# Norms between the matrix stages of a two-block transformer kernel, run in two token halves

## The reference, cut to what matters

```python
def rms_norm(x, g):
    return x * lax.rsqrt(jnp.mean(x * x, axis=-1, keepdims=True) + 1e-6) * g

def first_block(x, ...):
    x = x + 0.5 * g1 * swiglu(modulate(rms_norm(x, ffn1_norm), sh1, sc1), ...)      # FFN1
    h = modulate(rms_norm(x, mix_norm), sh2, sc2)                                   # norm 1
    x = x + g2 * (gated sum of a Fourier mix and a latent attention of h) @ w_out
    h = modulate(rms_norm(x, ffn2_norm), sh3, sc3)                                  # norm 2
    x = x + 0.5 * g3 * swiglu(h, ...)                                               # FFN2
    return rms_norm(x, final_norm)                                                  # norm 3

def second_block(x, ...):
    h = rms_norm(x, g_pre_mix) * (1 + sc1) + sh1                                    # norm 4
    o = concat(nsa_attention(h @ w_in ...), dsa_attention(...)) @ w_out
    x = x + gt1 * rms_norm(o, g_post_mix)                                           # norm 5
    h = rms_norm(x, g_pre_ffn) * (1 + sc2) + sh2                                    # norm 6
    y = square(relu(h @ w_up)) @ w_down                                             # FFN3
    return x + gt2 * rms_norm(y, g_post_ffn)                                        # norm 7
```

## Time and profile before

| | us |
|---|---|
| median of 3 runs | 2074.18 (2074.07 to 2074.76) |
| the profiled execution | 2074.3 |
| its span, first to last instruction | 2072.5 |
| TensorE (PE) busy | 1936.2 (93%) |
| DVE busy | 1212.3 (58%) |
| POOL busy | 1150.9 (56%) |
| ACT busy | 363.2 (18%) |
| chain that ended last: share of PE, DVE | 86%, 10% |

### The profile page before, as it was taken

One profiled execution on the slowest core, in us unless ns is written; L12 is line 12 of the kernel. 1 busy time (PEld: TensorE's weight loads), 2 busy tenths in 40 slices (PEclk: granted clock), 3 DMA queues, 4 the chain that ended last, 5 costly groups with the idle time before them and its releaser, 6 DMA issues.

```text
span 2072.5 us, 25215 instructions
## 1 busy us (share of the span) xinstructions
PE 1936.2 (93%) x8980; PEld 1526.7 (74%) x8980; DVE 1212.3 (58%) x1822; ACT 363.2 (18%) x749; POOL 1150.9 (56%) x1075
## 2 busy tenths in 40 slices
PE   6999999989899999899999978985999979999997
PEld 3788888868657888788888847664666748788785
DVE  7888478746644124887078355675774367405713
ACT  2100000022145111200000031112555230000001
POOL 3577777756440667576777643575000338767861
PEclk8999999999999999999999989896999989999998
DMA  8654555422220234454355221233000112233231
GB/s 277 203 175 158 189 167 183 151 85 89 64 62 1 62 102 140 129 189 132 118 191 172 89 68 41 81 72 93 1 1 1 41 41 87 95 101 94 89 101 40
DMA packets 231130, 216.51 MB, mean 104 GB/s; under 512 B 20305, under 2 KB 227342, under 8 KB 231054
## 3 DMA queue, kind: packets, MB, share of 16 engines
q1 hardware_dynamic: 230000, 214.84, 32.7%
q10 hardware_dynamic: 1054, 0.66, 0.1%
HBM read 213.39 MB, written 2.10 MB: 104 GB/s over the span
## 4 chain that ended last, share of the span: by engine, by line
PE 86%; DVE 10%; ACT 1%; issue 1%; POOL 1%; DMA 0%; ACTq 0%; DVEq 0%; POOLq 0%; SPq 0%
PE ps L614 24%; PE ps L616 24%; PE ps L615 23%; PE ps L891 5%; PE ps L914 4%; PE ps L900 3%; DVE rb L1437 1%; PE ps L660 1%; DVE tt L1931 1%; DVE tt L1654 1%; DVE xT L1932 1%; DVE ada_sum L1466 1%; DVE score L1815 1%; PE ps L645 1%; PE ps L851 0%
## 5 line engine op out<-in xcount | busy, mean ns | idle before, releaser
L525 POOL TENSOR_TENSOR w_lo<-raw,w_hi 128x512 fp32r<-128x512 f32 (+2 forms) x612 | 798.7, 1335 | 12.8
L614 PE MATMUL ps<-h_hi,w_hi 128*128 128x512 f32 x1424 | 565.6, 397 | 28.1 <-DVE h_lo L1459 26.7
L615 PE MATMUL ps<-h_lo,w_hi 128*128 128x512 f32 x1424 | 557.7, 392 | 0.0
L616 PE MATMUL ps<-h_hi,w_lo 128*128 128x512 f32 x1424 | 557.6, 392 | 0.0
L518 POOL TENSOR_TENSOR w_hi<-raw,ones 128x8 fp32r<-128x8 f32 x153 | 34.6, 226 | 870.1 <-PE ps L616 820.5
L614 PEld LDWEIGHTS ps<-h_hi,w_hi 128*128 128x128 f32 x1424 | 269.5, 189 | 92.0 <-issue 35.1
L1466 DVE SCALAR_TENSOR_TENSOR ada_sum<-ada,cT,ada_sum 128x256 f32<-128x256 f32 x378 | 325.1, 860 | 13.4
L615 PEld LDWEIGHTS ps<-h_lo,w_hi 128*128 128x128 f32 x1424 | 269.5, 189 | 58.0 <-issue 2.4
L616 PEld LDWEIGHTS ps<-h_hi,w_lo 128*128 128x128 f32 x1424 | 269.1, 189 | 57.8
L614 PE MATMUL ps<-g_hi,w_hi 128*128 128x512 f32 x608 | 237.4, 390 | 3.1 <-ACT sg L1396 3.1
L616 PE MATMUL ps<-g_hi,w_lo 128*128 128x512 f32 x608 | 236.7, 389 | 0.0
(11 more groups left out here) (274 smaller groups left out, 2239.3 us busy)
## 6 DMA issues: line engine op xcount, KB each, us to landing
ada<-in_ada_w SPq DMA_DIRECT2D x31, 1024.0 KB, 5.3
ada<-in_w_ada SPq DMA_DIRECT2D x24, 1024.0 KB, 6.6
raw<-in_ffn_w_gate SPq DMA_DIRECT2D x22, 1024.0 KB, 6.8
raw<-in_ffn_w_up SPq DMA_DIRECT2D x22, 1024.0 KB, 5.1
raw<-in_w_in SPq DMA_DIRECT2D x16, 1024.0 KB, 5.1
raw<-in_w_up SPq DMA_DIRECT2D x16, 1024.0 KB, 5.2
raw<-in_w_down SPq DMA_DIRECT2D x16, 1024.0 KB, 5.0
raw<-in_ffn_w_down SPq DMA_DIRECT2D x16, 768.0 KB, 4.3
```

The source lines that it names most:

```text
L525: last = pool.tensor_tensor(lo[:, c], src[:, c], hi[:, c].bitcast(F32), ALU.subtract)
L614: pe.matmul(o, wh, xh, start=start, stop=False)
L615: pe.matmul(o, wh, xl, start=False, stop=False)
L616: return pe.matmul(o, wl, xh, start=False, stop=stop)
```

## The change

Tokens 0 to 255 are half 0, tokens 256 to 511 half 1 (`HALF`). Two new functions on TensorE, with their counterparts on ACT (`boundary_high`) and DVE (`boundary`), replace the end of a stage and the start of the next:

- `last_pair`: output chunks 6 and 7 are computed for half 0 first, from the stage's last tile or last two tiles, then for half 1; the norm's sum of half 0 (`half_sum`) stands between the products of half 1.
- `first_tiles`: the first two tiles of the next stage are applied to half 0, then to half 1; the sum of half 1 stands after the fourth row chunk of the first of these tiles.
- DVE and ACT do the norm's root, reciprocal, scaling and split with 256 columns at a time; the reciprocal of half 1 stands in DVE's queue between the chunks of half 0.

This is done at norms 1, 2 and 4, and at norms 5 and 6 (there norm 6's sum over half 1, `mid_sum(1)`, stands behind half 0 of both first tiles); at norm 7 only the end of the stage is in halves, and the result is stored in halves, two chunks to a DMA.

Norms 3 and 4 are one: the root of mean(x²·g²) + 1e-6·(mean(x²) + 1e-6) is written as a sum of squares weighted by `gain2` = g² + 1e-6, and only one reciprocal goes into the scaling. The output of norm 3 itself, which the residual of block 2 needs, is computed later (`block1_root`, `block1_out`), between DVE's rotations and selections. For that TensorE does the plain sum of squares once more behind `first_tiles` of this norm (`y_sum`).

The first tile of each of the four stages behind such a norm (`EXTRA`: W_MIX, W_FFN2, W_IN2, W_FFN3) has a slot of its own (`we_hi`, `we_lo`); the other tiles alternate between the two old slots. The second tile of the stage goes into the slot of the tile two before it, as before, and the third tile into the slot of the last tile of the stage that ends. The rotations of `qi`, `kd` and `ki` move between the four token chunks of `nat`.

```diff
+EXTRA = (W_MIX, W_FFN2, W_IN2, W_FFN3)
...
+    we_hi = place("we_hi", [P, SLOT], F32R, at=at(20))
+    we_lo = place("we_lo", [P, SLOT], F32R, at=at(52))
...
+    def place_of(n):
+        return (n - sum(e < n for e in EXTRA)) % 2
...
+    def last_user(n):
+        return max(k for k in range(n) if k not in EXTRA and place_of(k) == place_of(n))
...
-            if not first:
+            if per:
                 pool.wait_ge(tile_used, i * per + (n - 1))
+            elif n in EXTRA:
+                pool.wait_ge(tile_used, n - 3)
+            elif not first:
+                pool.wait_ge(tile_used, last_user(n) + 1)
...
+        def last_pair(i, tiles, kc, xh, xl, ready=lambda u: None):
+            for u, n in enumerate(tiles):
+                pe.wait_ge(split_done, n + 1)
+                ready(u)
+                for m in range(2):
+                    last = part(ps[:, 2 + m, HALF[0]], n, kc, m, xh, xl, kc * u, HALF[0], u == 0, n == tiles[-1])
+                    if n == tiles[-1]:
+                        last.then_inc(half_mm, 1)
+            for u, n in enumerate(tiles):
+                for m in range(2):
+                    last = part(ps[:, 6 + m, HALF[1]], n, kc, m, xh, xl, kc * u, HALF[1], u == 0, n == tiles[-1])
...
+                    if m == 1:
+                        last.then_inc(tile_used, 1)
+                    if u == 0 and m == len(tiles) - 1:
+                        half_sum(i, 0)
+        def first_tiles(n0, banks, a0, b0, between, after=lambda: None, first_done=None):
+            for h in range(2):
+                t = HALF[h]
+                for u in range(2):
+                    n = n0 + u
+                    pe.wait_ge(split_done, n + 1)
+                    wh, wl = slot(w_hi, n, NC, 256), slot(w_lo, n, NC, 256)
+                    for k in range(NC):
+                        pe.wait_ge((lo_a, h_lo_done)[h], (a0, b0)[h] + k + 1)
...
+                        if h == 0 and u == 0 and k == 3:
+                            between()
+                    if h == 1:
+                        last.then_inc(tile_used, 1)
+                if h == 0:
+                    after()
...
-        norm_sum(5)
-        norm_sum(6)
+        pe.wait_ge(y_ready, 4)
+        last_pair(N_POST2, (W_OUT2 + 3,), NC, h_hi, h_lo)
+        half_sum(N_POST2, 1)
+        mid_sum(0)
...
+        def boundary(i, add, factor, shift, a0, b0):
+            for m in range(ON_DVE, NC):
+                add(m, 0)
+                if m == ON_DVE:
+                    norm_add(i, ON_DVE - 1)
+            half_inverse(i, 0)
+            half_scaled(0, 0, factor, a0)
+            add(ON_DVE, 1)
+            for m in range(1, NC + 1):
+                if m < NC:
+                    half_scaled(m, 0, factor, a0)
+                half_low(m - 1, 0, shift, a0)
+                if m == 2:
+                    add(ON_DVE + 1, 1)
+                if m == 6:
+                    half_inverse(i, 1)
+            for m in range(NC + 1):
...
+        block1_root()
         for i in range(4):
             rotate2(4 + i, qn[:, i])
+            block1_out(i)
             select(2)
```

More of the change, by code:

```diff
@@ L289, in build, with squares @@
     ident = kst[:, K_ID:K_ID + P]
[L291 removed]
     ON_DVE = NC - 2
+    HALF = (slice(0, T // 2), slice(T // 2, T))
+    N_FFN1, N_MIX, N_FFN2, N_PRE2, N_POST2, N_PRE3, N_POST3 = range(7)
+    SUMMED = (N_FFN1, N_MIX, N_FFN2, N_PRE2, N_POST2, N_POST3)
     def added(i, m):
[L297 removed]
+        return ON_DVE * SUMMED.index(i) + m + 1
     def last_added(i):
[L300 removed]
+        return added(i, ON_DVE - 1)
+    def squares(i):
+        return 8 * SUMMED.index(i)
     block = ctx.enter_context(nc.Block())
@@ L538, in _ @@
                     split(1, NC, 256, first=True)
-                with pool.Fori(1 if n0 == 0 else 0, iters) as it:
+                elif n0 == W_FFN2:
+                    for u in range(4):
+                        split(n0 + u, NC, 256)
+                with pool.Fori({0: 1, W_FFN2: 2}.get(n0, 0), iters) as it:
                     for u in range(2):
@@ L546, in _ @@
             n0 = W_FFN3 + 16 * half
-            with pool.Fori(0, 4) as it:
+            if half == 0:
+                for u in range(4):
+                    split(n0 + u, NC, 256)
+            with pool.Fori(2 - 2 * half, 4) as it:
                 for u in range(2):
@@ new lines, in mid_sum, with part @@
+        def mid_sum(h):
+            t = HALF[h]
+            for m in range(NC):
+                pe.wait_ge(mid_sq, NC * h + m + 1)
+                last = pe.matmul(ps[:, B_ADA, t], ones[:], sq[:, m % 2, t], start=m == 0, stop=m == NC - 1)
+                last.then_inc(mid_acc if m < NC - 1 else (sum_a, n_sum)[h], 1)
+        def part(o, n, kc, m, xh, xl, k0, t, start, stop):
+            wh, wl = slot(w_hi, n, kc, 256), slot(w_lo, n, kc, 256)
+            c = slice(P * m, P * m + P)
+            for k in range(kc):
+                last = mm3(o, wh[:, k, c], wl[:, k, c], xh[:, k0 + k, t], xl[:, k0 + k, t],
+                           start and k == 0, stop and k == kc - 1)
+            return last
@@ L748, in run_ffn @@
                 pe.wait_ge(mod_read, (4, 5, 7, 7)[2 * i + half])
-                first = i == 0 and half == 0
-                if first:
-                    gate_up(0, 0, 0, tiles=(1,))
-                with pe.Fori(int(first), iters) as it:
+                if half == 0:
+                    if i == 0:
+                        gate_up(0, 0, 0, tiles=(1,))
+                    else:
+                        first_tiles(n0, (0, 1, 2, 3), 8, 16, lambda: half_sum(N_FFN2, 1))
+                        for u in range(2):
+                            ada_mm_step(s0 + u)
+                with pe.Fori(1 - half, iters) as it:
                     gate_up(i, half, it)
@@ new lines, in run_ffn @@
+                if half == 0:
+                    with pe.Fori(0, 2) as jj:
+                        for jo in range(2):
+                            down_pair(jo, jj)
+                        if i == 0:
+                            pe.wait_ge(mod_read, 5)
+                            for u in range(2):
+                                ada_mm_step(s0 + 2 * iters + u, jj, 2)
+                else:
+                    for j in range(3):
+                        down_pair(j)
+                        if i == 0 and j:
+                            for u in range(2):
+                                ada_mm_step(s0 + 2 * iters + 2 * j - 2 + u)
+                    pe.wait_ge(x_ready, x0 + 4)
+                    last_pair((N_MIX, N_PRE2)[i], (n1 + 6, n1 + 7), iters, g_hi, g_lo)
@@ L975, in _ @@
                     signal(last, wo_mm, i, 2)
-        for i in range(2, 8):
+        for i in range(2, 6):
             n = W_OUT + i // 2
@@ L1113, in _ @@
         pe.wait_ge(o_lo_done, 12)
-        for i in range(8):
+        for i in range(6):
             n = W_OUT2 + i // 2
@@ new lines, in _ @@
+            if half == 0:
+                with pe.Fori(0, 2) as jj:
+                    for jo in range(2):
+                        down_pair(jo, jj)
+            else:
+                for j in range(3):
+                    down_pair(j)
+                pe.wait_ge(y_ready, 20)
+                last_pair(N_POST3, (n1 + 6, n1 + 7), NC, g_hi, g_lo)
+        half_sum(N_POST3, 1)
+        for h in range(2):
+            for m in range(NC):
+                pe.wait_ge(end_x, NC * h + m + 1)
+                if NC * h + m >= 2:
+                    pe.wait_ge(out_ev, NC * h + m - 1)
+                for c in range(2):
+                    last = pe.transpose(ps[:, m % 2, P * c:P * c + P], xT[:, m, P * (2 * h + c):P * (2 * h + c) + P], ident)
+                last.then_inc(out_tr, 1)
@@ L1159, in norm_squares @@
+    def norm_squares(act, i, ready, first, src, chunks=range(NC)):
+        for m in chunks:
             act.wait_ge(ready, first + m + 1)
```

445 lines of the change are left out of this document (294 added, 151 removed).

## The result

The changed kernel took **2094.95 us** (median of 4 runs, 2093.15 to 2095.38) against 2074.47 before (2074.07 to 2081.41): ratio 1.0087, 95% interval 1.0070 to 1.0103. Slower by 0.9%, where 2079.0 was forecast with a range of 2060 to 2088. The sign was right; the size was over four times the forecast (20.5 us for 4.7) and outside the range. The profiled execution took 2095.38 us with a span of 2093.6, 21.1 more than that of before. The runs of the kernel before fall in two groups, near 2075 us with a mean granted clock near 0.966 and near 2080 us with 0.961, so kernels that ran on different chips are compared by their ratio to it and not by their medians.

The account below looks back on a forecast made before the run. PE, 93% busy, was taken as the bound; only its waits and slow running could be won. Norm 2 +3.5, norm 1 +5.2, norms 3/4 -7.7, norms 5/6 +3.3, norm 7 +0.5 sum to 4.8: 2079.0 us, range 2060 to 2088.

Parts of the forecast that it names:

- norm 2, step by step: From zero, the last tile's start, to the next two tiles' end: 46.8 us against 44.4, plus 1 for clock: +3.5.
- turns of DVE and POOL: Under POOL's third tile, two-SBUF-input DVE operations alternate with POOL's: 1.2 to 1.4 us each, for 256 or 512 columns.
- Root 0.7 and half a reciprocal 1.7.: Norm 2: after half 0's sum ends at 10.0 us, root and half reciprocal are done at 12.4.
- Norms 5 and 6, +3.3.: From the last tile's start to the second next tile's end: 64.1 us against 62.1, plus 1.3 for clock.
- two half reciprocals and the last square: 30.4: Norms 5 and 6: after eight chunks end at 26.7 us, these finish at 30.4; first `h_lo` at 32.0.
- Norms 3 and 4, -7.7 with the rotations.: Fused norm wins 9.4 us up to the index scores; 1.7 are given back ahead of `blk_lo`.
- two of 0.7 to 1 us ahead of the chain to `blk_lo`: Two of eight `block1_out` delay the chain to `blk_lo`, on which PE waits: 1.7 us given back.
- Norm 1, +5.2.: Both next tiles end 53.7 us after the last tile's start, against 48.5, including a new 3.0 us wait for POOL.
- POOL does not bite: Rival, 0.30, 2046 to 2069 us: POOL's third tile comes after DVE's chunks or turns cost less; 2054, half effect 2067.
- The clock stays low: Rival, 0.15, 2084 to 2092 us: half products of `first_tiles` at 0.50 clock cost some 3 us per stage; 2087.
- Gains and losses cancel: Rival, 0.15, within 4 us of 2074: the fused norm wins 12 instead of 7.7 and pays for the four others.
- price of half products: In `last_pair` and `first_tiles`, 696 products halved, two halves costing 0.013 us more than a whole: 9.2 us of PE time.

Follow-up runs that it names:

- experiment 2: Changed kernel with POOL starting the third tile behind norms 1, 2, 3/4 and 5/6 only after the first half's last low part; 2081.66 us, ratio 1.0022.
- Experiment 1: Changed kernel with the two waits ahead of each first half root written in the other order; 2090.31 us, ratio 1.0061.
- experiment 3: Changed kernel with both second-half copies (chunks 6 and 7) ahead of norm 5's first normed chunk in DVE's queue; 2092.34 us, ratio 1.0067.
- experiment 5: Changed kernel with norms 5 and 6, the last tile ahead and the first two tiles behind in full width again; 2086.02 us, ratio 1.0042.
- experiment 4: Changed kernel with the last three scalings of block 1's output moved behind the last blk_lo; 2091.3 us, ratio 1.0060.
- edits 1 to 4: Root's waits swapped, POOL's third tile after the first half's low parts, both copies first at norm 5, last three scalings late; together 2076.6 us.
- experiment 6: Changed kernel with root's waits swapped, POOL's third tile delayed, both copies first at norm 5 and last three scalings late; 2076.6 us, ratio 0.9992.
- experiment 7, second run: Kernel before the change with only norms 3 and 4 made one, in full width, no halves, run again; 2069.84 us, ratio 0.9963.

## Why the prediction was wrong

Held: the sign; norm 2, step by step (+3.3 for +3.5); the **turns of DVE and POOL**, taken at 1.2 to 1.4 us each (the six operations under POOL at norm 5 took 7.2 us, the six at norm 2 7.1, so 1.2 each); norm 7 (46.8 to 47.8 us from the start of its last pair, +1.0 for +0.5); that the last rotation would stand at the end of the chain to the index scores (PE waits 4.51 us for it). Of the observations named as proof, POOL was at work where it stood still, and the last tile's wait on `w_lo` was 3.22 us at norm 4 and 2.43 at norm 7, but 0.64 at norm 1. In norm 2 there is some luck: its first `h_lo` was done 17.2 us after zero (823.13), not 15.7, since the table load below stood in the way; but POOL's third tile was through at 21.1, and the fourth `h_lo` came at 22.7, to the tenth as forecast. Not held: the point of 1.1 us per operation under POOL, below which the kernel was to be faster than before. With 0.42 to 0.48 us per operation in half 0 (experiment 2) it was still 0.2% slower.

Wrong, by the steps of the prediction:

- **"Root 0.7 and half a reciprocal 1.7."** The root was taken to follow the sum as in the earlier trace rows. The order of two waits put the table load of 1.28 us between them at four norms. Experiment 1 gives back 4.6 us. No term of the sum held it. The source showed that the two waits had changed places; that the load goes with the one written last is seen only in the traces.
- **Norms 5 and 6, +3.3.** Measured from their zero (1666.7): first product 35.4 us after it (forecast 32.0), half 0 done 49.3 (46), next product 58.2 (51.1), and the end of the two tiles 71.1 (64.1). The term "two half reciprocals and the last square: 30.4" took the squares of norm 6 to follow DVE's chunks; they stood behind norm 5's second half in ACT's queue (experiment 3: 3.7 us of the first product). And "sum, root, reciprocal of norm 6" was to be hidden behind half 0's products, but PE itself does that sum, after them: 4.82 us, then root, reciprocal and first chunk, 8.9 us from the last product of half 0 to the first of half 1 where 5.1 were forecast. A further 1.5 us came ahead of the zero, with PE at 1.2 GHz for 3.4 us of the W_OUT tiles. Full width takes 8.6 back (experiment 5).
- **Norms 3 and 4, -7.7 with the rotations.** 4.3 us late already where the two first tiles end (1264.1, 58.7 after the zero of 1205.4, forecast 54.4; experiment 1 gave back 2.3 us of this stretch, experiment 2 4.5); from there it went as forecast, 34.1 us for 34.1 to the scores. The term "two of 0.7 to 1 us ahead of the chain to `blk_lo`" missed the third, and that one of them took 1.77 under POOL: 1.6 us more (experiment 4). The remaining 0.6 us of the miss of 2.2 are not told apart.
- **Norm 1, +5.2.** The mean of its two profiles is +5.6 (100.0 and 103.5 against 96.1). That this is near the forecast is luck, since single terms were off and balanced: the wait for the last tile's split was 0.64 us and not 3.0, and another of 1.23 for a sum of DVE's (`ada_sum`) and the table load came in its place.

The **rivals**. *POOL does not bite* (2054) was wrong by more than a part: with POOL kept off half 0 the kernel took 2081.7, since the other causes stay. *The clock stays low* (2087) had a true core: the mean granted clock fell from 0.966 to 0.960 of the span, 2 x (0.040 x 2093.6 - 0.034 x 2072.5) = 27 us more at 1.2 GHz (the lower level is half the upper), which can have cost 13 us at most, and less wherever DVE sets the pace. Three of these stretches (us; busy PE, PEld, DVE, ACT, POOL; granted clock):

```profile
1683.60:1697.30 13.70, 8.33 (x19) 4.35 (x18) 10.52 (x16) 4.00 (x10) 4.21 (x4) 0.51 0.36 111
434.30:444.50 10.20, 9.13 (x32) 7.76 (x33) 7.34 (x12) 2.57 (x6) 5.56 (x6) 0.50 0.66 204
1700.70:1707.50 6.80, 5.39 (x26) 5.42 (x27) 6.37 (x15) 3.85 (x8) 0.00 (x0) 0.51 0.00 0
```

How much of the 21 us it makes was not tried; fillers in the halved kernel, whose rests are many and short, would be one way. *Gains and losses cancel* (2074) would have needed a fused norm worth 12 us; alone it is worth 5 to 8 by the ratios.

Experiments 1 to 4 gave 4.6, 13.3, 2.6 and 3.7 us by the medians, 24 in all, or 21 if only the stretches that they aim at are counted for the last two (1.4 and 1.6). Together they gave 18.4 (2094.95 to 2076.6; 18.7 to 19.7 by the ratios), so they overlap by 2 to 6 us.

What is left after them shows in PE's own time, by the pages (us):

| | span | PE busy | PE's rest |
|---|---|---|---|
| before | 2072.5 | 1936.2 | 136.3 |
| changed | 2093.6 | 1959.5 | 134.1 |
| changed, with edits 1 to 4 (experiment 6) | 2077.2 | 1957.5 | 119.7 |
| fused norm alone (experiment 7, second run) | 2066.6 | 1937.5 | 129.1 |

The four edits took 14.4 us of rest away and almost no busy time. Against the fused norm alone, the mended halves have 9.4 us less rest, which is what halving was meant to bring, and 20.0 us more busy time. The 9.2 us of the price of half products are in that: in the changed kernel they follow each other at 0.120 us (twelve of them from 2045.78 to 2047.22), as forecast. The mean clock does not explain the rest (0.963 and 0.964). Since the ends of products are modelled, a part may be the way of counting. The other 10.8 us are not told apart, and halves of products were not tried alone.

## What to carry to other kernels

Halving a step shortens the way to the first result only if what runs beside it halves too: here a DVE operation under POOL took 1.2 us for 256 columns and 1.65 for 512, so two halves took half as long again as the whole. Before costing such a change, list for each engine's queue what a new instruction stands behind (ACT's squares behind a root, PE's sum behind products, a table load behind a wait), since each halved norm has twice as many of these places. And try the parts alone: the fused norm without halves was 0.3 to 0.4% faster than before, with the halves 0.8 to 0.9% slower. Look at an engine's busy time as well as at its waits: here the halves saved 9 us of PE's rest once all was mended, and cost 20 us of its work.
